# Two-layer decoder trunk on one core: first weight units by quarters, one dense step per attention turn, output norm from PSUM, four weight splits on GpSimd

## The chip, the cores and the metric

The kernel runs on one core of a Trainium2 chip. The metric is the device time of one execution in microseconds; the time before is the median of 3 runs. One further execution was taken with the hardware profiler; all rows below are of that one. Engines are named as in the profile: PE (TensorE matmul), DVE (VectorE), ACT (ScalarE), POOL (GpSimd), SP (the queue that issues the loads).

## The reference, cut to what matters

512 tokens of width 1024 pass two layers. Layer 0 mixes tokens by sliding-window attention with a learned sink per head (16 query heads, 4 key heads of 64 columns, blocks of 128 tokens; a block sees itself and the block before). Layer 1 scores keys with a small indexer (8 heads), keeps the best 128 keys per query among the causal ones, and attends to those. After each mixer comes a squared-ReLU MLP of width 4096. Each sub-layer is normed on its way in and on its way out:

```python
for layer in range(2):
    g = norm_gains[layer]
    hn = rmsnorm(x, g[0])
    mix = sliding_window_sink_attention(hn, ...) if layer == 0 else dsa_sparse_attention(hn, ...)
    x = x + rmsnorm(mix, g[1])
    hn = rmsnorm(x, g[2])
    x = x + rmsnorm(squared_relu_mlp(hn, w_mlp_up[layer], w_mlp_down[layer]), g[3])
```

Everything is float32.

## The kernel before, in words

**Products.** A float32 product is made of three matmuls on values that are split in a high and a low part (`dense`, L1396, and `three`, L1391). A *unit* is 512 rows by 512 columns of a weight matrix, 1 MB. SP loads unit `u` into one of two buffers `w_raw` (`load`, L364) and waits before that until the low part of unit `u - 2` is made. ACT makes the high part (`split`, L606), in four pieces of 512 columns with the norm's gain, or in one of 2048 where there is no gain; only after the last piece it says so, and then DVE makes the low part (`split`, L934). PE waits for `w_lo_done`. A *dense step* is one unit against one block of 128 tokens: 4 row blocks times 3 matmuls of 512 columns. Two steps (h = 0, 1) give a tile of the input projection (`in_work`, L1407) or of the output projection (`out_work`, L1443).

**Order.** Every engine has its order of work written out by hand and runs it in that order; a wait holds all that is behind it on the engine. Semaphores count what is done. SP issues the loads in the order of the units: layer 0 input projection (units 0 to 5), output projection (6 to 9), MLP (10 to 41), indexer queries (42, 43) and keys (44), layer 1 input (45 to 50), output (51 to 54), MLP (55 to 86).

**Start.** SP issues blocks 0 and 1 of x, units 0 and 1, then blocks 2 and 3 of x. PE transposes each x block (`new_x`, L1457); ACT and DVE take the high and low part (`high`, L630; `low`, L955). The first dense steps wait for the whole of unit 0. Unit 2 reuses the place of unit 0, so its split waits for unit 0's last step (`w_before`, L289; `w_spent`, L305).

**Attention.** Both layers run 16 turns (pairs of heads, one query block each) in one loop that every engine walks (`attention`, L570, L732, L1043, L1575). In turn `n` PE transposes the probabilities of turn `n - 1` (`transposes`, L1549), makes the scores of turn `n + 1` (`scores`, L1527), runs the dense steps that the table `FILL` gives to the turn (L74; steps of the input projection first, then of the output projection), turns the queries or new x blocks of the tables `Q_TURN` and `H_TURN`, and multiplies by the values (`weighted`, L1559). DVE takes in turn `n` the reciprocal of the row sums of turn `n` (`inverse`, L1031), then masks the scores of turn `n + 1` (`masked`, L1014); then come the low parts of queries and x blocks, the splits of the turn, and in layer 1 rounds of the top-k search (`more_rounds`, L1324; a round is MAX8 and MATCH_REPLACE8 over the scores). ACT copies transposed probabilities, takes the exponentials of turn `n + 1` (`expo`, L709), scales queries (`q_scaled`, L677), then high parts and splits. POOL multiplies the probabilities by the reciprocals (`normed`, L505) and rotates queries (`rope_q`, L496). The sets `{0: (5,), 5: (6,), ...}` that the three attention calls are given (L847, L919) say which unit is split at the end of which turn.

**Output norm.** After an output tile, DVE copies it out of PSUM (`y_copied`, L975), ACT squares the copy (`y_square`, L659), POOL multiplies the left half by the gain (`gained`, L513), DVE the right half (`gained`, L982), DVE adds up the squares (`mean_square`, L994), POOL takes the inverse root (`rstd_y`, L520), DVE updates X (`x_update`, L1004). After the MLP the same is done on the sum in SBUF.

**Out tail and MLP.** `out_tail` (L1624) runs the last three output tiles with `new_x` of block 2 between them; `mlp` (L1631) runs four quarters of 1024 hidden columns, the first with its up-projection in halves (`up_half`, L1637) and `new_x` of block 3 after the first of them. Between layers (L1742 to L1758) come `new_x` of blocks 1 to 3, 8 steps of indexer queries (`qi_work`), the indexer keys (`ki_work`, `ki_tokens`, `ki_back`) and the index scores (`index`).

## Time and profile before

| | |
|---|---|
| median of 3 runs | 1232.45 us (1231.23 to 1232.61) |
| the profiled execution, its own time | 1233.58 us |
| its span (first to last instruction) | 1231.8 us |
| mean granted TensorE clock | 0.968 |
| PE busy | 1133.5 us, 92% |
| DVE, ACT, POOL busy | 619.6, 452.3, 165.9 us |

A row of the timeline gives start and length in us, engine, line, operation, and in square brackets how long the engine was idle before it and what ended that. The views by stage give the busy time of each engine in a stretch and PEclk, the TensorE clock granted there as a share of the full one: 1.00 is the upper level (2.4 GHz) throughout, 0.50 would be the lower level (1.2 GHz) throughout. "Modelled ends" means that a busy PE is not always a PE at its peak. A share of busy time over the whole span mixes stages with different limits, so stages are read one at a time.

### The profile page before, as it was taken

To read this page: it belongs to the slowest core of one execution; us is meant where nothing else is said; L and a number is where in the kernel's file an instruction comes from. 1 tells how busy PE (TensorE), PEld (TensorE's weight loads), DVE (VectorE), ACT (ScalarE), POOL (GpSimd) and SP (SyncE) were. 2 spreads that over 40 slices of the span, in tenths; PEclk is the share of its full clock that TensorE was granted. 3 is DMA by queue.
4 is the path that set the end of the run, shared out by engine and by line. 5 is a ranking of instruction groups with operands and counts; after the bars stand their busy time and mean duration, and the time that the engine had idled before them with its cause. 6 is when DMAs were issued, how large, how long until landed. Compare 5 with 4: busy or idle time off the path is not lost.

```text
span 1231.8 us, 15111 instructions
## 1 busy us (share of the span) xinstructions
PE 1133.5 (92%) x5577; PEld 909.5 (74%) x5577; DVE 619.6 (50%) x1125; ACT 452.3 (37%) x854; POOL 165.9 (13%) x323
## 2 busy tenths in 40 slices
PE   4979898999999999999899848888999999999996
PEld 3867576888888888887677626555888888888885
DVE  3234553543553453557387786453552453553454
ACT  4446663323322322334454344363323221322322
POOL 0224341000000000002313222351000000000002
PEclk9989999999999999999999878899999999999999
DMA  8221411424444443443314132000515444344431
GB/s 208 65 58 34 103 35 35 103 58 113 88 101 103 102 102 84 94 96 79 86 35 99 39 88 51 1 1 5 125 43 120 103 90 103 83 101 102 103 69 68
DMA packets 50719, 97.72 MB, mean 79 GB/s; under 512 B 4384, under 2 KB 4576, under 8 KB 50656
## 3 DMA queue, kind: packets, MB, share of 16 engines
q1 hardware_dynamic: 50144, 96.78, 34.8%
q8 instruction: 38, 0.62, 0.2%
q10 hardware_dynamic: 512, 0.11, 0.1%
q14 instruction: 25, 0.20, 0.1%
HBM read 94.78 MB, written 2.10 MB: 79 GB/s over the span
## 4 chain that ended last, share of the span: by engine, by line
PE 77%; DVE 11%; ACT 6%; issue 3%; DMA 2%; POOL 1%; SPq 0%; DVEq 0%; POOLq 0%; ACTq 0%
PE bank L1393 9%; PE bank L1394 9%; PE bank L1392 9%; PE bank L1693 9%; PE bank L1692 9%; PE bank L1691 9%; PE bank L1402 6%; PE bank L1403 5%; PE bank L1404 5%; PE bank L1503 2%; PE bank L1556 2%; DVE score L1106 2%; PE bank L1570 2%; DVE top L1101 2%; DVE w_lo L951 1%
## 5 line engine op out<-in xcount | busy, mean ns | idle before, releaser
L951 DVE SCALAR_TENSOR_TENSOR w_lo<-w_raw,gT,w_hi 128x512 fp32r<-128x512 f32 x164 | 112.8, 750 | 174.3 <-ACT w_hi L626 174.2
L1691 PE MATMUL bank<-w_hi,r_hi 128*128 128x512 f32 x512 | 199.7, 390 | 0.0
L1693 PE MATMUL bank<-w_hi,r_lo 128*128 128x512 f32 x512 | 199.4, 389 | 0.0
L1692 PE MATMUL bank<-w_lo,r_hi 128*128 128x512 f32 x512 | 199.4, 389 | 0.0
L1392 PE MATMUL bank<-r_hi,w_hi 128*128 128x512 f32 (+1 forms) x456 | 178.1, 390 | 0.0
L1393 PE MATMUL bank<-r_hi,w_lo 128*128 128x512 f32 (+1 forms) x456 | 177.9, 390 | 0.0
L1394 PE MATMUL bank<-r_lo,w_hi 128*128 128x512 f32 (+1 forms) x456 | 177.9, 390 | 0.0
L626 ACT ACTIVATE w_hi<-w_raw,gT 128x512 fp32r<-128x512 f32 x164 | 105.0, 712 | 188.4 <-PE bank L1693 103.7
L941 DVE TENSOR_TENSOR w_lo<-w_raw,w_hi 128x2048 fp32r<-128x2048 f32 x36 | 82.5, 2292 | 128.6 <-ACT w_hi L618 128.6
L1402 PE MATMUL bank<-w_hi,r_hi 128*128 128x512 f32 x272 | 116.3, 427 | 16.7 <-DVE w_lo L951 9.4
L618 ACT ACTIVATE w_hi<-w_raw 128x2048 fp32r<-128x2048 f32 x36 | 68.9, 1913 | 156.1 <-PE bank L1693 118.7
L1691 PEld LDWEIGHTS bank<-w_hi,r_hi 128*128 128x128 f32 x512 | 96.4, 188 | 20.0
L1692 PEld LDWEIGHTS bank<-w_lo,r_hi 128*128 128x128 f32 x512 | 96.4, 188 | 20.0
L1693 PEld LDWEIGHTS bank<-w_hi,r_lo 128*128 128x128 f32 x512 | 96.2, 188 | 20.0
L1403 PE MATMUL bank<-w_lo,r_hi 128*128 128x512 f32 x272 | 110.6, 407 | 0.0
L1404 PE MATMUL bank<-w_hi,r_lo 128*128 128x512 f32 x272 | 110.6, 407 | 0.0
L1392 PEld LDWEIGHTS bank<-r_hi,w_hi 128*128 128x128 f32 (+1 forms) x456 | 85.5, 188 | 18.3 <-issue 0.4
L1394 PEld LDWEIGHTS bank<-r_lo,w_hi 128*128 128x128 f32 (+1 forms) x456 | 85.4, 187 | 18.3 <-issue 0.4
L1393 PEld LDWEIGHTS bank<-r_hi,w_lo 128*128 128x128 f32 (+1 forms) x456 | 85.4, 187 | 18.2 <-issue 0.4
L511 POOL TENSOR_TENSOR probs<-probs,small 128x256 f32<-128x256 f32 (+3 forms) x128 | 78.3, 643 | 112.8 <-DVE small L1034 112.7
L783 ACT ACTIVATE r_hi<-tmp_b 128x512 fp32r<-128x512 f32 x64 | 40.4, 632 | 143.6 <-DVE tmp_b L1166 143.6
L717 ACT ACTIVATE probs<-probs,small 128x257 f32<-128x257 f32 (+5 forms) x128 | 65.5, 513 | 70.1 <-DVE small L1027 69.3
(152 smaller groups left out, 1581.8 us busy)
## 6 DMA issues: line engine op xcount, KB each, us to landing
w_raw<-in_w_mlp_up SPq DMA_DIRECT2D x64, 512.0 KB, 5.9
w_raw<-in_w_mlp_down SPq DMA_DIRECT2D x64, 512.0 KB, 6.4
w_raw<-in_b_w_in SPq DMA_DIRECT2D x16, 512.0 KB, 6.1
w_raw<-in_a_w_in SPq DMA_DIRECT2D x12, 512.0 KB, 6.8
w_raw<-in_a_w_out SPq DMA_DIRECT2D x8, 512.0 KB, 5.7
w_raw<-in_b_w_out SPq DMA_DIRECT2D x8, 512.0 KB, 5.8
X<-in_x SPq DMA_DIRECT2D x4, 512.0 KB, 10.1
G<-in_norm_gains SPq DMA_DIRECT2D x4, 512.0 KB, 7.4
```

Source lines behind the costliest of these rows:

```text
L626: last = nc.scalar.activation(w_h[:, cs], w_raw[:, slot, cs], ACT.Copy, scale=gain(layer, 2 if name[:3] == "mlp" else 0, 4 * (n % 2) + k))
L941: last = nc.vector.tensor_tensor(w_l, w_raw[:, slot, :], w_h.bitcast(f32), ALU.subtract)
L951: last = nc.vector.scalar_tensor_tensor(out=w_l[:, cs], in0=w_raw[:, slot, cs], scalar=g, in1=w_h[:, cs].bitcast(f32), op0=ALU.mult, op1=A ...
L1392: nc.tensor.matmul(bank, whi, xhi, start=start, stop=False)
L1393: nc.tensor.matmul(bank, wlo, xhi, start=False, stop=False)
L1394: return nc.tensor.matmul(bank, whi, xlo, start=False, stop=stop)
L1402: nc.tensor.matmul(bank[:], xh, hi[:, k, :], start=h == 0 and k == 0, stop=False)
L1403: nc.tensor.matmul(bank[:], xh, lo[:, k, :], start=False, stop=False)
L1404: ins = nc.tensor.matmul(bank[:], xl, hi[:, k, :], start=False, stop=h == 1 and k == 3)
L1691: nc.tensor.matmul(bank[:], xh, hi[:, k, :], start=h == 0 and k == 0, stop=False)
L1692: nc.tensor.matmul(bank[:], xh, lo[:, k, :], start=False, stop=False)
L1693: ins = nc.tensor.matmul(bank[:], xl, hi[:, k, :], start=False, stop=h == 1 and k == 3)
```

## The change: what it does

1. **Start.** Units 0 and 1 are loaded and split by quarters (128 rows each, a semaphore for each); PE takes the steps of token blocks 0 and 1 quarter by quarter (`start_work`). The transposes of block 2 stand inside unit 1's steps, those of block 3 after step 4. ACT squares x blocks between the pieces.
2. **Attention.** `FILL` gives (nearly) each turn one dense step; queries and x blocks are turned right after the scores instead of before the last value product, and their high and low parts are made before the exponentials and after the first masks. DVE takes the reciprocal of turn `n + 1` at the end of turn `n`, before splits and top-k rounds, where it was the first thing in turn `n + 1`. Splits have a table (`SPLITS`), at most one a turn; unit 4's split goes behind the first queries.
3. **GpSimd** makes the low parts of layer 1's output units 51 to 54, four pieces each (`split_low`), where DVE did.
4. **Output norm.** ACT squares the output tile straight from PSUM, DVE multiplies it by the gain straight from PSUM (`out_gained`); the copy and POOL's and DVE's gain products of these tiles are gone. After the MLP, POOL makes both gain products, save one.
5. **Ends.** The out tail runs its six steps in one row, then `new_x` of block 2; `new_x` of block 3 stands inside the second `up_half`. The last down-projection finishes blocks 0 and 1 earlier. Between the layers unit 43's split (in a place of its own) goes behind two square sums on ACT and before the last X update on DVE, and the steps of indexer queries, keys and input projection are reordered.

```diff
+FILL = ({-1: (0, 1), 0: (2, 3), 1: (4,), 2: (5,), 3: (6,), 4: (7,), 5: (8,), 6: (9,), 7: (10,), 8: (11,),
+         9: (12,), 10: (13, 14), 11: (15, 16), 12: (17, 18), 13: (19,), 14: (20,), 15: (21,)},
+        {0: (0,), 1: (1,), 3: (2,), 4: (3,), 5: (4,), 6: (5,), 7: (6,), 8: (7,), 10: (8,), 11: (9,), 12: (10,), 13: (11,),
+         14: (12,), 15: (13,)})
+Q_TURN = ({-1: ((1, 0), (1, 1)), 1: ((1, 2),), 2: ((1, 3),), 4: ((2, 0),), 5: ((2, 1),), 8: ((2, 2),), 9: ((2, 3),)},
+          {-1: ((2, 0),), 0: ((2, 1),), 4: ((2, 2),), 5: ((2, 3),)})
+H_TURN = ({13: (0,), 15: (1,)}, {10: (0,), 15: (1,)})
+SPLITS = ({-1: (4,), 1: (5,), 6: (6,), 8: (7,), 9: (8,), 10: (9,)}, {1: (51,), 4: (52,), 5: (53,), 6: (54,)})
+POOL_UNITS = (51, 52, 53, 54)
...
-            load_in(0, 0)
-            load_in(0, 1)
+            for u in range(2):
+                for k in range(4):
+                    r0 = 512 * u + P * k
+                    sp.dma_start(w_raw[:, u, 512 * k:512 * k + 512], a_in[r0:r0 + P, QD:QD + 512]).then_inc(start_in[4 * u + k], 16)
...
+            def split_low(u):
+                w_h, w_l = (t.rearrange("p (k n) -> p k n", k=4) for t in w_place(u))
+                raw = w_raw[:, u % 2, :].rearrange("p (k n) -> p k n", k=4)
+                pool.wait_ge(w_hi_done, hi_no(u))
+                for k in range(4):
+                    nc.gpsimd.tensor_tensor(w_l[:, k, :], raw[:, k, :], w_h[:, k, :].bitcast(f32), ALU.subtract).then_inc(out_lo_done, 1)
...
                     if 0 <= n < TURNS:
                         normed(layer, n)
+                    for j in pending:
+                        rstd_y(norm, j)
+                    pending = []
+                    for u in SPLITS[layer].get(n - 1, ()):
+                        if u in POOL_UNITS:
+                            split_low(u)
...
                 if norm % 2:
-                    act.wait_ge(y_out, 8 * (norm // 2) + 2 * j + c + 1)
+                    d = d_no(norm // 2, "out", c, j)
+                    act.wait_ge(d_done, d + 1)
+                    v = banks[d_bank(norm // 2, d)][:]
...
+                    for c, j in Q_TURN[layer].get(n, ()) if n >= 0 else ():
+                        q_high(layer, q_no(layer, c, j))
+                    for j in H_TURN[layer].get(n, ()):
+                        high(norm, j)
                     if n + 1 < TURNS:
                         expo(layer, n + 1, 0)
                         expo(layer, n + 1, 2)
...
+            def out_gained(layer, j, c):
+                norm = 2 * layer + 1
+                dve.wait_ge(sq_done, 8 * (norm - 1) + 2 * j + c + 1)
+                dve.wait_ge(post_gain_in, 16 * norm)
                 if j >= 2:
-                    dve.wait_ge(x_new, 16 * layer + 2 * (j - 2) + c + 1)
-                nc.vector.tensor_copy(yb[:, j % 2, 512 * c:512 * c + 512], banks[d_bank(layer, d)][:]).then_inc(y_out, 1)
+                    dve.wait_ge(x_new, 8 * (norm - 1) + 2 * (j - 2) + c + 1)
+                cs = slice(512 * c, 512 * c + 512)
+                nc.vector.tensor_tensor(yb[:, j % 2, cs], banks[d_bank(layer, d_no(layer, "out", c, j))][:], G[:, cs],
+                                        ALU.mult).then_inc(y_out, 1)
...
-                    if 0 <= n < TURNS:
-                        inverse(layer, n)
                     for j in pending:
                         mean_square(norm, j)
+                    first = (0, 1, 2, 3) if n + 1 < TURNS and width(layer, turn(layer, n + 1)[1]) <= 256 else (0, 1)
                     if n + 1 < TURNS:
-                        masked(layer, n + 1)
+                        masked(layer, n + 1, first)
+                    for c, j in Q_TURN[layer].get(n, ()) if n >= 0 else ():
+                        q_low(layer, q_no(layer, c, j))
+                    for j in H_TURN[layer].get(n, ()):
+                        low(norm, j)
+                    if n + 1 < TURNS and len(first) == 2:
+                        masked(layer, n + 1, (2, 3))
                     for j in pending:
                         x_update(norm, j)
...
+                    if n == -1 and not layer:
+                        split(4)
+                    if n + 1 < TURNS:
+                        inverse(layer, n + 1)
+                    for u in SPLITS[layer].get(n, ()) if n >= 0 else ():
+                        if u not in POOL_UNITS:
+                            split(u)
                     others(n)
...
+            ROUNDS_3 = (0, 1, 3, 5, 7, 9, 11, 12, 13, 15, TOPK // 8)
...
+            def start_work():
+                for u, order in ((0, ((0, 0), (0, 1), (1, 0), (1, 1), (0, 2), (1, 2), (0, 3), (1, 3))),
+                                 (1, tuple((j, k) for j in range(2) for k in range(4)))):
...
+                        pe.wait_ge(start_lo_done, 4 * u + k + 1)
...
                     if n + 1 < TURNS:
                         scores_of(n + 1)
+                    turned(n)
                     for s in FILL[layer].get(n, ()):
                         fill(s)
                     for c in range(Ks):
-                        if c == max(0, Ks - 2):
-                            turned(n)
                         weighted(layer, n - 1, c)
...
-                    if (j, c) == (3, 0):
-                        new_x(2 * layer + 1, 2)
+                new_x(2 * layer + 1, 2)
...
+                    if end:
+                        steps = [(0, 0), (0, 1), (0, 2), (1, 0), (1, 1), (0, 3), (1, 2), (1, 3)]
...
             new_x(2, 1)
             qi_work(0, 0)
-            qi_work(0, 1)
             new_x(2, 2)
             qi_work(1, 0)
+            qi_work(0, 1)
+            qi_work(1, 1)
             new_x(2, 3)
-            qi_work(1, 1)
+            qi_work(2, 0)
             queries_turned(1, 8)
+            qi_work(2, 1)
+            queries_turned(1, 9)
             ki_work()
-            queries_turned(1, 9)
-            qi_work(2, 0)
+            qi_work(3, 0)
             ki_tokens()
-            qi_work(2, 1)
-            qi_work(3, 0)
+            qi_work(3, 1)
             queries_turned(1, 10)
             ki_back()
-            qi_work(3, 1)
+            in_work(1, 0)
             index(0)
```

## Rows read from the trace of the kernel before

**Rows 1.** The page, busy time of each engine, share of the span, instructions.
```profile
PE 1133.5 (92%) x5577; PEld 909.5 (74%) x5577; DVE 619.6 (50%) x1125; ACT 452.3 (37%) x854; POOL 165.9 (13%) x323
```

**Rows 2.** By stage: length, then busy PE, PEld, DVE, ACT, POOL, then PEclk, DMA.
```profile
0.00:94.00 94.00, 69.03 (x315) 55.25 (x316) 31.42 (x80) 43.03 (x88) 18.84 (x61) 0.95 0.47 113
94.00:186.00 92.00, 85.63 (x557) 63.06 (x556) 48.47 (x148) 58.95 (x158) 39.95 (x84) 0.98 0.23 53
186.00:230.00 44.00, 37.87 (x208) 31.66 (x207) 19.04 (x31) 15.93 (x31) 5.98 (x8) 0.92 0.21 48
230.00:560.00 330.00, 330.00 (x1514) 275.68 (x1513) 160.20 (x199) 93.20 (x120) 6.42 (x7) 1.00 0.45 97
560.00:615.00 55.00, 48.01 (x222) 37.54 (x222) 27.57 (x51) 22.94 (x49) 12.26 (x29) 0.94 0.31 72
...
689.00:848.00 159.00, 122.99 (x704) 81.82 (x702) 92.10 (x248) 78.11 (x200) 51.85 (x77) 0.87 0.12 27
848.00:881.00 33.00, 27.88 (x157) 24.52 (x156) 15.84 (x25) 11.79 (x23) 2.39 (x3) 0.95 0.27 64
...
1214.00:1231.80 17.80, 8.39 (x38) 6.60 (x36) 11.78 (x20) 2.89 (x8) 2.19 (x4) 0.83 0.31 118
```

**Rows 3.** The chain of waits: one 512-column matmul, upper clock level.
```profile
186.88 0.23 PE bank L1402
```

**Rows 4.** Timeline of the start, ACT and PE.
```profile
13.37 2.56 ACT L626 ACTIVATE w_hi<-w_raw,gT 128x512 fp32r<-128x512 f32 x4 [2.75 <-DMA w_raw<-in_a_w_in]
18.09 2.56 ACT L626 ACTIVATE w_hi<-w_raw,gT 128x512 fp32r<-128x512 f32 x4 [1.20 <-DMA w_raw<-in_a_w_in]
18.76 0.80 PE L1402 MATMUL bank<-w_hi,r_hi 128*128 128x512 f32 x1 [6.10 <-DVE w_lo L951]
30.54 1.62 PE L1469 MATMUL bank<-ident,X 128*128 128x128 f32 x8 [2.61 <-DVE r_lo L961]
```

**Rows 5.** Timeline, ACT and PE, first turn of layer 0's attention.
```profile
67.90 2.56 ACT L626 ACTIVATE w_hi<-w_raw,gT 128x512 fp32r<-128x512 f32 x4 [5.30 <-PE bank L1404]
73.97 0.47 PE L1503 MATMUL bank<-k_hi,r_hi 64*128 64x128 f32 x2 [6.17 <-DVE r_lo L972]
```

**Rows 6.** Timeline, PE, layer 0's turn 9.
```profile
136.80 2.31 PE L1556 MATMUL bank<-ident,probs 128*128 128x128 f32 x8 [3.78 <-POOL probs L511]
```

**Rows 7.** Timeline, PE, between the layers.
```profile
570.38 1.97 PE L1469 MATMUL bank<-ident,X 128*128 128x128 f32 x8 [2.31 <-DVE X L1011]
```

**Rows 8.** Groups by line, shapes apart: busy us, mean ns, idle before.
```profile
L941 DVE TENSOR_TENSOR w_lo<-w_raw,w_hi 128x2048 fp32r<-128x2048 f32 x36 | 82.5, 2292 | 128.6 <-ACT w_hi L618 128.6
L518 POOL TENSOR_TENSOR yb<-yb,G 128x512 f32<-128x512 f32 x8 | 10.3, 1284 | 47.9 <-ACT waste L668 47.9
```

**Rows 9.** Timeline, DVE, POOL and PE in one turn of layer 1.
```profile
727.79 0.18 DVE L1034 RECIPROCAL small<-small 128x4 f32<-128x4 f32 x1
728.05 2.33 POOL L511 TENSOR_TENSOR probs<-probs,small 128x256 f32<-128x256 f32 x4 [8.74 <-DVE small L1034]
730.52 1.09 PE L1556 MATMUL bank<-ident,probs 128*128 128x128 f32 x4 [6.81 <-POOL probs L511]
```

**Rows 10.** Timeline, DVE and POOL at once, then DVE alone, between the layers.
```profile
553.52 5.89 DVE L951 SCALAR_TENSOR_TENSOR early_lo<-w_raw,gT,early_hi 128x512 fp32r<-128x512 f32 x4 [0.16 <-ACT early_hi L626]
554.18 6.38 POOL L518 TENSOR_TENSOR y<-y,G 128x512 f32<-128x512 f32 x4 [269.72 <-ACT waste L668]
563.84 2.74 DVE L951 SCALAR_TENSOR_TENSOR w_lo<-w_raw,gT,w_hi 128x512 fp32r<-128x512 f32 x4 [4.42 <-ACT w_hi L626]
```

**Rows 11.** The page's groups: busy us, mean ns, the exponentials of both layers.
```profile
L717 ACT ACTIVATE probs<-probs,small 128x257 f32<-128x257 f32 (+5 forms) x128 | 65.5, 513 | 70.1 <-DVE small L1027 69.3
```

**Rows 12.** Timeline, DVE, the last norm, first and last token block.
```profile
1214.27 0.69 DVE L1177 TENSOR_TENSOR y<-y,bank 128x512 f32<-128x512 f32 x1 [9.30 <-PE bank L1693]
1225.51 0.68 DVE L1177 TENSOR_TENSOR y<-y,bank 128x512 f32<-128x512 f32 x1
```

**Rows 13.** Groups by line, shapes apart: the masks of layer 0.
```profile
L1027 DVE CUSTOM_DVE_ANT_0 probs<-bank,band,small 128x256 f32<-128x256 f32 x48 | 20.3, 478 | 8.5 <-PE bank L1503 8.5
```

More of the change, by code:

```diff
@@ L283, in w_place @@
                 return tuple(t[:] for t in early[n])
-            if name == "qi" and n == 0:
-                return tuple(t[:] for t in early[1])
-            s = {"qi": 0, "ki": 1}.get(name, u % 2)
+            if name == "qi":
+                return tuple(t[:] for t in early[1]) if n == 0 else (qi1_hi[:], qi1_lo[:])
+            s = 1 if name == "ki" else u % 2
             return w_hi[:, s, :], w_lo[:, s, :]
@@ L318, in w_spent, with hi_no, lo_no, low_of @@
             return d_done, d_no(layer, name[:-1], n // 2, 3) + 1
+        def hi_no(u):
+            return u - 1
+        def lo_no(u):
+            return u - 1 - sum(v < u for v in POOL_UNITS)
+        def low_of(u):
+            if u < 2:
+                return start_lo_done, 4 * u + 4
+            if u in POOL_UNITS:
+                return out_lo_done, 4 * POOL_UNITS.index(u) + 4
+            return w_lo_done, lo_no(u)
         def halves(w):
@@ L730, in o_high, with attention @@
                     "p (r n) -> p r n", r=4), ACT.Copy).then_inc(o_hi_done, 1)
-            def attention(layer, splits):
+            def attention(layer):
                 norm = 2 * layer + 1
@@ L740, in attention @@
                             q_high(layer, q_no(layer, c, j))
+                        for u in SPLITS[layer].get(n, ()):
+                            split(u)
                     if n == 0 and not layer:
@@ L761, in attention @@
                                 y_square(norm, j, c)
-                    for c, j in Q_TURN[layer].get(n, ()) if n >= 0 else ():
-                        q_high(layer, q_no(layer, c, j))
-                    for j in H_TURN[layer].get(n, ()):
-                        high(norm, j)
-                    for u in splits.get(n, ()):
+                    for u in SPLITS[layer].get(n, ()) if n >= 0 else ():
                         split(u)
@@ L802, in quarter @@
                             y_square(2 * layer + 2, j, 0)
-                        if not layer:
-                            split(U["qi"] + 1)
                     else:
@@ L1018, in masked @@
                 mask = own if i == 0 else score[:, i - 1, 0:W] if layer else band[:]
-                if n >= 3 or layer:
+                if es[0] == 0 and (n >= 3 or layer):
                     dve.wait_ge(pt_ready, PT_AT[N - 2])
-                for e in range(4):
+                for e in es:
                     rr, a = e // 2, e % 2
@@ L1041, in o_low, with attention @@
                                         hi.bitcast(f32), ALU.subtract).then_inc(o_lo_done, 1)
-            def attention(layer, splits, others):
+            def attention(layer, others):
                 norm = 2 * layer + 1
@@ L1081, in attention @@
                 x_update(norm, 2)
-                y_copied(layer, 3, 0)
+                out_gained(layer, 3, 0)
+                split(U[f"mlp{layer}"] + 1)
+                out_gained(layer, 3, 1)
+                mean_square(norm, 3)
                 low(norm, 2)
-                y_copied(layer, 3, 1)
-                gained(norm, 3)
-                mean_square(norm, 3)
-                split(U[f"mlp{layer}"] + 1)
                 x_update(norm, 3)
@@ L1604, in attention @@
                         turned(n)
-                    for s in FILL[layer][n][1:] if n == 0 else ():
-                        fill(s)
+                        for s in steps[1:]:
+                            fill(s)
                 for n in range(1, 17):
@@ L1649, in up_half @@
                                     h == 0 and k == 0 and m % 2 == 0, h == 1 and k == 3 and m % 2 == 1)
+                        if not half and h and n == 3:
+                            new_x(norm, 3)
                         if half and h == 0 and n == 15:
@@ L1701, in quarter @@
                         up_half(0, 0)
-                        new_x(norm, 3)
                         up_half(1, 0)
@@ L1710, in quarter @@
                     up(1, 1, it)
-                    for c in range(2):
-                        for h in range(2):
-                            for j in range(NB):
-                                down(c, h, j, it, first)
-                                if end and not layer and (c, h, j) == (1, 1, 2):
-                                    new_x(2, 0)
+                    steps = [(h, j) for h in range(2) for j in range(NB)]
+                    for h, j in steps:
+                        down(0, h, j, it, first)
+                    if end:
+                        steps = [(0, 0), (0, 1), (0, 2), (1, 0), (1, 1), (0, 3), (1, 2), (1, 3)]
+                    for h, j in steps:
+                        down(1, h, j, it, first)
+                        if end and not layer and (h, j) == (1, 2):
+                            new_x(2, 0)
                 quarter(0, True)
```

304 lines of the change are left out of this document (165 added, 139 removed).

## The prediction, made before the change was run

> **What bounds the kernel now.** First the page: PE is busy for 1133.5 of 1231.8 us [rows 1]; no other engine comes near. So I read what PE lacks, stage by stage, from the busy times by stage [rows 2]. The MLP of layer 0 (230 to 560) has PE busy all 330 us at the upper clock level, and 881 to 1214 reads the same: the change can win nothing in these 663 us. PE idles 25.0 us in the first 94, 6.4 in the rest of layer 0's attention, 6.1 in its out tail, 7.0 between the layers, 36.0 in layer 1's attention, 5.1 in its out tail and 9.4 at the end; the 3.3 that are left of 1231.8 - 1133.5 = 98.3 lie between 615 and 689. The column PEclk adds a second loss: a stage of length L at mean clock c spent 2(1-c)L at the lower level, where a matmul takes twice as long, so up to (1-c)L went there: 4.7, 1.8, 3.5, 3.3 and 1.7 us in five stages and 20.7 in layer 1's attention. These stages hold PE waits of 2 us and more [rows 4 to 7]; whether each wait that goes takes a slow stretch with it is open, so I count only part.
>
> No matmul is added or removed. The question is which waits go and which come. A dense step is 12 matmuls of 0.23 us [rows 3], 2.75 us; I use it as the measure of cover. A change under 0.2% (2.5 us) could not be told from none.
>
> **Start (0 to 94).** Units 0 and 1 land 4.7 us apart (ACT starts on them at 13.37 and 18.09 [rows 4]), so a quarter lands every 1.2 us and the first at about 9.8 (estimate). ACT needs 0.64 for a quarter, DVE 0.69 (a fourth of 2.56 [rows 4] and of 2.74 [rows 10]): the first matmul can run near 11.3 instead of 18.76, 7.4 us sooner, and six matmuls a quarter (1.4 us at the upper level, 2.8 at the lower) keep PE supplied. The 2.61 us before block 3's transposes [rows 4] go, as other steps stand there now. The 6.17 us at the first scores [rows 5] go: they were the split of unit 4, which held ACT and DVE from 67.90 with the first queries behind it, and now stands behind these. A wait comes: unit 2's split may start only after step 5, and one dense step and two key transposes (about 3.5 us) stand before its first use, where a second dense step stood too; ACT's 2.56 and then DVE's 2.74 make 5.3, so 2 us of wait. Of the clock's 4.7 I take 2. Eight DMAs instead of four on SP delay x blocks 2 and 3 by perhaps 2 us; both are needed after 20, so nothing. 7.4 + 2.6 + 6.2 - 2 + 2 = 16; bounds 10 (unit 2 twice as late, no clock) and 20.
>
> **Rest of layer 0's attention.** 3.78 us before turn 9's transposes [rows 6] come where no dense step stood in turn 8; now one stands in every turn. What is late next: at turn 9 the output projection needs the last low part of the values, which DVE makes behind unit 7's split, 2.29 us [rows 8] that wait for ACT's part first. The price lies between nothing and twice 2.29; some 3 us of PE work cover it, so I take 2. Queries turned right after the scores have one value product and one transpose less as cover: 0 to 2. Of 6.4 idle I take 4; bounds 0 and 7.
>
> **Out tails (186 to 230, 848 to 881).** The idle of 6.1 and 5.1 us [rows 2] lies where `new_x` of blocks 2 and 3 stands in PE's order while DVE and ACT still norm that block, behind a split each. Now three output tiles, 16.5 us, cover block 2, and the first `up_half` (48 matmuls at half of 0.23, 5.5 us) with the transposes covers block 3's norm, some two splits' worth (2 x 2.74 [rows 10]). That ACT and DVE read the tile in PSUM holds its bank longer, but two dense steps pass before it is needed: nothing; without them it would be the square and the product, about 1.5. Next late is block 3's update, by under 1. Of 6.1 + 3.5 I take 8 (bounds 5 and 9.6), of 5.1 + 1.7 6 (bounds 4 and 6.8).
>
> **Between the layers.** 2.31 us [rows 7]: DVE's split of unit 43 (at 563.84 [rows 10]) stood ahead of all norms; it goes behind three of them. New waits: the third indexer tile needs a bank whose eviction on ACT now stands behind block 3's high parts; the third query turn stands behind the rotation of the keys, which starts a dense step later. Each lies between nothing and a dense step, 2.75; I take 2.3 for the first, where more stands ahead, and 1.3 for the second. POOL's second gain product, 1.28 [rows 8], stands before its inverse root, where DVE took about half: 0.7. Of 7.0 + 3.3 that leaves 5; the index and top-k rounds after it are paced by DVE, so 4, bounds 1 and 8.
>
> **Layer 1's attention (689 to 848).** In turn 5 the reciprocal ran at 727.79, behind a split of 2.29 us [rows 8] and two top-k rounds; POOL had been idle 8.74, PE waited 6.81 [rows 9]. Now the reciprocal stands before both, and the four splits (4 x 2.29 = 9.2 us) leave DVE. It pays with waiting for exponentials: four take 2.05 [rows 11] while the masks run beside them, so I put 0.9 us a turn, 14 in all. DVE's 92.1 - 9.2 + 14 = 97 stays under PE's work: 41 us were at the lower level, 77% of them busy, worth 16, so 123 - 16 = 107. Walking the turns with these lengths (an estimate) I find PE still waiting for 17: 1.3 to 2 in each of the first turns, where top-k rounds stand between two masks and there is little dense work, 3.1 in turn 5 (values behind the rounds), 3.9 in turn 9. POOL takes 4 x 1.28 = 5.1 for a split and 2.33 for a turn's products [rows 8, 9], 7.4 against a turn of 6.4: units 53 and 54 come up to 3 us late, counted in the 17. Add 6 for slow clock after waits and 10 for what a walk does not find: 107 + 17 + 6 + 10 = 140 of 159, gain 19; bounds 6 (half the idle comes back) and 30.
>
> Here the trace and a rule of the Trainium skill are weighed. POOL's four products and DVE's four pieces of a split ran at once: DVE took 5.89 where it takes 2.74 alone, POOL 6.38 where four alone take 5.14 [rows 8, 10]. So each stops the other. In the turns that get POOL's splits DVE runs masks and low parts from PSUM and top-k rounds on one SBUF operand, so I add nothing. The Trainium skill, SBUF — State Buffer, "Who interferes with whom", says that a DVE instruction with two SBUF inputs and a GpSimd instruction that reads SBUF lock each other out; by that rule, X updates beside POOL's new gain products would be held, which is a rival below. The Trainium skill, GPSIMD Engine Reference, "4.1 Engine selection", speaks against the move: two-input elementwise work belongs on VectorE, being about twice as slow on GpSimd. The trace agrees, 5.14 against 2.29; the sum has that price, as POOL's time, not PE's.
>
> **End.** Token blocks cost DVE 3.75 us each in a row (1214.27 to 1225.51 for three [rows 12]) though PE ends sooner. Now blocks 0 and 1 end one dense step earlier and POOL makes three gain products: the last block starts when block 2 is done, about 1.7 sooner; bounds 0 and 2.
>
> **Sum.** 16 + 4 + 8 + 6 + 4 + 19 + 1.7 = 58.7. The profiled execution took 1233.58 us, its span 1231.8, the median 1232.45; so 1231.8 - 58.7 = 1173.1, plus 1.8 around the span, minus 1.1 from the profiled run to the median: 1174. All lower bounds together (26) give 1206, all upper ones (83) 1149.
>
> **Rivals.** (a) *DVE becomes the pacer of the turns.* It now stops for exponentials, and in out-projection turns for the dense step and the square, before the reciprocal; speaking for it are 92.1 busy us in that stage [rows 2] and the 2.05 of exponentials. If the 14 us lie on its path, layer 1 gains 5 instead of 19: 1188. (b) *The lock between DVE and POOL.* The X updates between the layers and at the end wait for the seven gain products that are new on POOL: 7 x 1.28 = 9, 1183. Against it: DVE adds from PSUM or waits for POOL's root while most of them run. (c) *Slower.* Each of 32 turns becomes a chain: masks 4 x 0.48 = 1.9 [rows 13], rest of the exponentials 0.9, reciprocal 0.2, POOL 2.33 [rows 9]; 5.3 us, of which one dense step covers 2.75: 2.55 exposed, 32 x 2.55 = 82 against 58.7 won: 1256. It decides from 1.8 us a turn. Against it: scores are a full turn ahead. (d) *Nothing gained.* Waits only move to the next semaphore: 1232. Against it: rows 4, 5 and 9 name the instruction in the way, and each is moved off.
>
> **Chances.** Forecast 0.67, (a) 0.16, (b) 0.08, (c) 0.05, (d) 0.02, better than all bounds together 0.02. The range 1154 to 1204 holds the forecast, (a) and (b) with most of their bounds and leaves out the rest and both corners. Faster by over 0.2%: 0.93; within: 0.02; slower: 0.05.
>
> **What would show it.** The stages in the new profile: first dense matmul near 11; no idle over 3 us in layer 0's turns; PE idle in layer 1's attention near 20 instead of 36 and PEclk above 0.90 there; POOL near 20 us busier; MLP stretches unchanged at 100%. I am wrong if transposes wait for POOL in most turns, if PE waits for GpSimd's low parts by more than 3 us a unit, or if idle in the first 94 us stays over 18.

## The result, and the profile after

The changed kernel takes 1166.8 us (median of 4 runs, 1165.97 to 1167.3), the kernel before 1232.53 beside it: a ratio of 0.9468, interval 0.9456 to 0.9479. 1174 was predicted, with 1154 to 1204 as the range. The profiled execution took 1166.92 us, its span is 1165.1, the mean granted clock 0.985 (before 0.968). One run of b2 below (1313.36 us) and one of the kernel before beside it (1318.3) were in a slower state and are left out of the medians and ratios given here.

The page's busy times, changed kernel; they answer to [rows 1]:

```profile
PE 1116.0 (96%) x5577; PEld 896.5 (77%) x5577; DVE 600.7 (52%) x1106; ACT 450.2 (39%) x854; POOL 192.3 (17%) x338
```

PE's busy time fell by 17.5 us though it does the same matmuls: that is slow clock that went. Its idle time fell from 98.3 to 49.1, and POOL has 26.4 us more to do. By stage (length, then busy PE, PEld, DVE, ACT, POOL, then PEclk; cut where PE's work changes), to be read beside [rows 2]:

```profile
0.00:57.00 57.00, 48.40 (x221) 39.71 (x221) 21.41 (x45) 28.32 (x52) 12.77 (x43) 1.00 0.60 159
57.00:94.00 37.00, 35.51 (x240) 26.66 (x238) 20.72 (x77) 29.22 (x83) 18.77 (x46) 1.00 0.25 57
94.00:175.00 81.00, 75.34 (x459) 54.79 (x458) 38.75 (x107) 46.80 (x119) 32.85 (x58) 0.94 0.23 53
175.00:217.00 42.00, 42.00 (x284) 38.99 (x285) 23.49 (x38) 15.78 (x29) 1.09 (x2) 1.00 0.45 98
217.00:546.00 329.00, 329.00 (x1461) 272.64 (x1461) 160.64 (x203) 96.07 (x128) 12.62 (x13) 1.00 0.42 93
546.00:600.00 54.00, 48.25 (x250) 37.10 (x248) 27.93 (x58) 26.57 (x56) 15.92 (x34) 0.97 0.40 88
600.00:657.00 57.00, 53.67 (x248) 41.82 (x244) 45.34 (x105) 24.20 (x43) 14.51 (x32) 0.97 0.33 74
657.00:790.00 133.00, 116.56 (x712) 76.89 (x711) 82.46 (x244) 78.08 (x201) 69.56 (x94) 0.95 0.14 33
790.00:831.00 41.00, 41.00 (x281) 38.12 (x280) 22.91 (x37) 15.37 (x29) 1.09 (x2) 1.00 0.45 97
```

Both out tails and the MLP are full. What PE still lacks stands in the start (5.25 of 8.6 us there ahead of the first transposes, which wait for their constants), in the second half of layer 0's turns, between the layers, and above all in layer 1's turns, where 133 - 116.56 = 16.4 us are idle (36.0 before).

Fixed points of PE's work make the two kernels comparable: the start of the first score matmul of each layer, of its last value product, and of its first whole `up` matmul, from the rows of these three lines in the trace. Between the points, in us:

| stage | before | after | won | predicted |
|---|---|---|---|---|
| start, to layer 0's first scores | 74.0 | 56.8 | 17.2 | 16 |
| layer 0's turns | 120.0 | 117.8 | 2.2 | 4 |
| layer 0's out tail | 50.2 | 41.5 | 8.7 | 8 |
| MLP, between the layers, index | 445.4 | 443.8 | 1.6 | 4 |
| layer 1's turns | 157.6 | 129.3 | 28.3 | 19 |
| layer 1's out tail | 48.6 | 41.5 | 7.1 | 6 |
| MLP and end | 336.0 | 334.4 | 1.6 | 1.7 |

(One dense step of 2.75 us stands ahead of layer 1's first scores before and behind them after; the table counts it ahead in both.) The sum is 66.7 us of span, 58.7 were forecast. Of the 28.3 us in layer 1's turns, 19.6 are idle time that went; the rest is slow clock.

A stage of one profile is not sharp to a microsecond. Layer 0's turns are the same code in the changed kernel and in e1 below; they take 117.8 and 114.8 us, with 7.15 us of idle PE in both and a granted clock of 0.957 and 0.985. So where stages of two runs are compared below, PE's idle time stands beside them.

The first dense matmul runs at 10.11 instead of 18.76 [rows 4]. Waits left on PE that the prediction had spoken of, from the timeline:

```profile
10.11 0.78 PE L1497 MATMUL bank<-w_hi,r_hi 128*128 128x512 f32 x1
...
38.87 0.50 PE L1478 MATMUL bank<-w_hi,r_hi 128*128 128x512 f32 x1 [2.35 <-DVE w_lo L1013]
...
109.94 1.02 PE L1579 MATMUL bank<-ident,qs 128*128 128x128 f32 x4 [2.11 <-POOL qs L516]
...
121.00 0.77 PE L1478 MATMUL bank<-w_hi,r_hi 128*128 128x512 f32 x1 [1.86 <-DVE r_lo L1106]
...
558.75 0.47 PE L1478 MATMUL bank<-early_hi,r_hi 128*128 128x512 f32 x1 [1.41 <-ACT qs L741]
...
579.26 0.63 PE L1579 MATMUL bank<-ident,qs 128*128 128x128 f32 x4 [2.57 <-POOL qs L516]
```

38.87 is unit 2's split, 121.00 the values' low part behind unit 7's split, 558.75 the bank of the third indexer tile, 579.26 the third indexer query: the waits that were forecast (2, 2, 2.3, 1.3). 109.94 is a query step whose rotation on POOL comes late, just above the 0 to 2 that stood there. Ahead of the first transposes PE is idle longer (5.25 us); after that the longest wait is 2.75 us at 727.16, in layer 1's turns, for DVE's masks.

### The profile page after: what moved, and what is told of

It is laid out like the page before. It is cut to its first block and busy times, and to the rows that moved or that the text cites. A ratio compares the mean times of both kernels' runs of the same rounds, so it can differ in the third digit from the quotient of the medians.

```text
span 1165.1 us, 15098 instructions
## 1 busy us (share of the span) xinstructions
PE 1116.0 (96%) x5577; PEld 896.5 (77%) x5577; DVE 600.7 (52%) x1106; ACT 450.2 (39%) x854; POOL 192.3 (17%) x338
## 5 line engine op out<-in xcount | busy, mean ns | idle before, releaser
L1789 PE MATMUL bank<-w_hi,r_hi 128*128 128x512 f32 x512 | 199.3, 389 | 0.0
L1791 PE MATMUL bank<-w_hi,r_lo 128*128 128x512 f32 x512 | 199.2, 389 | 0.0
L1790 PE MATMUL bank<-w_lo,r_hi 128*128 128x512 f32 x512 | 199.2, 389 | 0.0
L1013 DVE SCALAR_TENSOR_TENSOR w_lo<-w_raw,gT,w_hi 128x512 fp32r<-128x512 f32 x152 | 104.5, 751 | 149.3 <-ACT w_hi L678 149.2
L678 ACT ACTIVATE w_hi<-w_raw,gT 128x512 fp32r<-128x512 f32 x152 | 97.1, 713 | 174.7 <-PE bank L1791 103.7
L1003 DVE TENSOR_TENSOR w_lo<-w_raw,w_hi 128x2048 fp32r<-128x2048 f32 x34 | 78.3, 2302 | 124.7 <-ACT w_hi L670 124.7
L1478 PE MATMUL bank<-w_hi,r_hi 128*128 128x512 f32 x240 | 103.1, 430 | 8.4 <-DVE w_lo L1013 6.5
L549 POOL TENSOR_TENSOR y<-y,G 128x512 f32<-128x512 f32 x8 | 13.0, 1652 | 537.1 <-ACT waste L723 537.1
L541 POOL TENSOR_TENSOR probs<-probs,small 128x256 f32<-128x256 f32 (+3 forms) x128 | 84.4, 690 | 89.7 <-DVE small L1100 89.7
L1479 PE MATMUL bank<-w_lo,r_hi 128*128 128x512 f32 x240 | 97.6, 407 | 0.0
L1480 PE MATMUL bank<-w_hi,r_lo 128*128 128x512 f32 x240 | 97.6, 407 | 0.0
```

Of the source, the lines that this page charges most:

```text
L541: nc.gpsimd.tensor_tensor(v, v, inv_sum[:, N % 3, c:c + 1].to_broadcast([P, W]), ALU.mult).then_inc(p_done, 1)
L678: last = nc.scalar.activation(w_h[:, cs], w_raw[:, slot, cs], ACT.Copy, scale=gain(layer, 2 if name[:3] == "mlp" else 0, 4 * (n % 2) + k))
L1013: last = nc.vector.scalar_tensor_tensor(out=w_l[:, cs], in0=w_raw[:, slot, cs], scalar=g, in1=w_h[:, cs].bitcast(f32), op0=ALU.mult, op1=A ...
L1478: nc.tensor.matmul(bank[:], xh, hi[:, k, :], start=h == 0 and k == 0, stop=False)
L1479: nc.tensor.matmul(bank[:], xh, lo[:, k, :], start=False, stop=False)
L1480: ins = nc.tensor.matmul(bank[:], xl, hi[:, k, :], start=False, stop=h == 1 and k == 3)
```

## The experiments

Layer 1's turns won half as much again as forecast, so the first question is which edit did it. One edit is taken back at a time (e1, e2, e8), or made alone on the kernel before (b1, b2, b3).

**Low parts of layer 1's output units back on DVE (e1).**

```diff
-POOL_UNITS = (51, 52, 53, 54)
+POOL_UNITS = ()
```

> The changed kernel, but the low parts of layer 1's four output units go back to DVE (2.29 us each there), behind the reciprocal and ahead of the next turn's masks. Theory A (the move to POOL is worth time, because DVE paces the turns with top-k rounds, and because a two-input subtraction on DVE stops POOL, as in layer 0's turn 8, where POOL's four products took 4.37 us beside a split and 2.33 us alone): 6 to 10 us slower than the changed kernel's 1166.8, so 1173 to 1177, with POOL's products near 4.4 us in the turns that have a split. Rival B (DVE had room, the move is worth nothing): 1165 to 1169, products at 2.33.

1181.53 us, ratio to before 0.9584 (0.9568 to 0.9601): 14.7 us lost, more than even theory A had; layer 1's turns take 148.6 instead of 132.1 us from first scores to last product. DVE's four splits, with what DVE idled ahead of them (us, times), and a timeline of POOL and DVE beside the second:

```profile
L1003 DVE TENSOR_TENSOR w_lo<-w_raw,w_hi x2: 2291/2404/2517, 676.0 to 698.0; 128x2048 fp32r<-128x2048 f32 x2
L1003 DVE TENSOR_TENSOR r_lo<-w_raw,r_hi x2: 2356/2371/2386, 708.5 to 718.8; 128x2048 fp32r<-128x2048 f32 x2
...
  ACT w_hi L670: 5.5, 2
  ACT r_hi L670: 2.7, 2
```

```profile
697.74 4.38 POOL L541 TENSOR_TENSOR probs<-probs,small 128x256 f32<-128x256 f32 x4
...
697.99 2.52 DVE L1003 TENSOR_TENSOR w_lo<-w_raw,w_hi 128x2048 fp32r<-128x2048 f32 x1 [2.33 <-ACT w_hi L670]
```

The four instructions run 9.6 us, and ahead of them DVE stands 5.5 + 2.7 = 8.2 us still until ACT has made the high part: 17.8 in all. A little of that standing takes the place of other waits: from first scores to last product DVE is busy 9.6 us longer (92.0 for 82.4) and idle 6.9 us longer (56.6 for 49.7), which together are the 16.5 us that the stage lost. On PE 10.9 of them are waits (27.4 us idle for 16.4); the rest is slow clock, 0.885 granted for 0.948. POOL's four products take 4.38 us beside a split in three turns of that width and 2.33 in the one without. PE's waits in layer 1's turns, first the changed kernel, then this one (total us, times, longest):

```profile
PE bank L1599 <- DVE small L1093: 6.9, 5, 2.7
PE bank L1579 <- POOL qs L516: 2.1, 1, 2.1
PE bank L1666 <- ACT pt L778: 2.1, 3, 1.3
PE bank L1652 <- POOL probs L541: 1.6, 2, 1.2
PE bank L1478 <- POOL r_lo L562: 1.2, 1, 1.2
```

```profile
PE bank L1599 <- DVE small L1093: 15.4, 5, 4.9
PE bank L1478 <- DVE r_lo L1106: 4.8, 1, 4.8
```

PE waits for masks (L1093) and for the values' low part (L1106): work of DVE that queues behind the splits. In the changed kernel the low parts that POOL makes come late once, by 1.2 us (the last line of the first list).

**The reciprocal back in the next turn (e2).** `inverse(layer, n)` ahead of turn n+1's masks, in both layers.

> The changed kernel with the reciprocal of a turn's sums back at the start of the next turn on DVE, so behind that turn's split and top-k rounds. Theory A (the reciprocal's place is the main part of layer 1's gain): 12 to 20 us slower than the changed kernel, 1179 to 1187, with PE waiting for POOL's products in layer 1's turns. Rival C (PE's new order and one dense step a turn bring the gain, and scores a turn ahead hide the reciprocal): 1167 to 1171.

1171.98 us (0.9504; 0.9486 to 0.9522): 5.2 lost, 3.5 of it in layer 1's turns (135.6). Theory A falls here, and its rival is nearer.

**The early reciprocal alone, on the kernel before (b1).**

```diff
-                    if 0 <= n < TURNS:
-                        inverse(layer, n)
...
+                    if n + 1 < TURNS:
+                        inverse(layer, n + 1)
                     for c, j in Q_TURN[layer].get(n, ()) if n >= 0 else ():
                         q_low(layer, q_no(layer, c, j))
```

> The kernel before, with one edit alone: the reciprocal stands ahead of the queries' low parts, the splits and the top-k rounds of the turn in which its exponentials run. Theory A: 10 to 18 us faster than the kernel before, 1214 to 1222, most of it in layer 1's attention. Rival C: 0 to 4 us, 1228 to 1232. If it is slower, DVE's waits for exponentials cost more than they give without the other edits.

1232.69 us, ratio 0.9998 (0.9987 to 1.0009): nothing. PE's waits in layer 1's turns, first the kernel before, then this one:

```profile
PE bank L1556 <- POOL probs L511: 16.9, 7, 6.8
PE bank L1402 <- DVE r_lo L1040: 5.6, 2, 4.6
PE bank L1503 <- DVE small L1027: 5.4, 5, 3.0
...
PE bank L1556 <- DVE r_lo L972: 0.2, 1, 0.2
```

```profile
PE bank L1503 <- DVE small L1027: 11.0, 8, 3.1
PE bank L1556 <- DVE r_lo L972: 6.6, 1, 6.6
PE bank L1402 <- DVE r_lo L1040: 5.7, 2, 4.7
...
PE bank L1556 <- POOL probs L511: 3.8, 5, 1.2
```

The 16.9 us of waiting for POOL's products shrank to 3.8, as meant, and came back as masks (5.4 to 11.0) and as the queries' low part (0.2 to 6.6). The rest of DVE's queue came hardly sooner. In turn 5 the next masks start at 727.91 in the kernel before and at 727.25 here; behind them come the exponentials and the high and low part of a query, and PE's second transposes wait for the bank that this low part frees. First the kernel before, then b1:

```profile
731.03 0.69 DVE L972 TENSOR_TENSOR r_lo<-bank,r_hi 128x512 fp32r<-128x512 f32 x1 [1.41 <-ACT r_hi L699]
731.77 1.11 PE L1556 MATMUL bank<-ident,probs 128*128 128x128 f32 x4 [0.16 <-DVE r_lo L972]
```

```profile
730.36 0.69 DVE L972 TENSOR_TENSOR r_lo<-bank,r_hi 128x512 fp32r<-128x512 f32 x1 [0.30 <-ACT r_hi L699]
731.11 1.11 PE L1556 MATMUL bank<-ident,probs 128*128 128x128 f32 x4 [6.59 <-DVE r_lo L972]
```

The low part was as late before; the wait of 6.81 us for the products [rows 9] hid it. (In b1 the reciprocal stands ahead of the queries' low parts, in the changed kernel behind them. At this wait that costs nothing, as the low part still waits 0.30 us for ACT.)

**The old fill in layer 1 (e8).** `FILL[1]`, `Q_TURN[1]`, `H_TURN[1]` and `SPLITS[1]` of the kernel before: two dense steps in some turns, none in others.

> The changed kernel with layer 1's turns filled as in the kernel before (up to two dense steps in a turn and none in others, with the turns of queries, blocks and splits that belong to it). Theory A: 3 to 8 us slower than the changed kernel, 1170 to 1175, the idle standing in the turns without a dense step. Rival C (the even fill is the main part): 12 to 20 us slower, 1179 to 1187.

1181.86 us (0.9582; 0.9563 to 0.9601): 15.1 lost. PE waits 3.9 us for POOL's products in one turn, 3.1 for a low part from POOL, 5.1 in all for values and 8.7 in all for masks: 24.6 us idle from first scores to last product for 16.4, and PEclk is 0.89 there (0.95 with the even fill). Rival C holds.

After these four I formed theory D: DVE's queue, its waits included, paces layer 1's turns. Two edits alone on the kernel before were to test it.

**Low parts on POOL alone (b2)**: `split_low` for units 51 to 54 behind the turn's products, nothing else.

> The kernel before, with one edit alone: POOL makes the low parts of layer 1's four output units, each behind its turn's products. Theory D (formed after the first runs: DVE's queue paces layer 1's turns; a low part costs it 2.29 us and the wait for ACT's high part ahead of it, 1.0 to 3.2 us, together some 17 us for four): 8 to 16 us faster than the kernel before, 1217 to 1225. Rival E (PE waits for POOL's products, 16.9 us in that stage, and POOL gets 20 us more to do): 1232 to 1238.

**The even fill alone (b3)**: `FILL[1]`, `Q_TURN[1]`, `H_TURN[1]` and the splits' turns of the changed kernel.

> The kernel before, with one edit alone: layer 1's turns filled as in the changed kernel (one dense step in a turn, with the turns of queries, blocks and splits that belong to it). Theory D (the cover is spread better, but DVE's queue is as long as it was): 3 to 8 us faster, 1225 to 1230. Rival F (the fill is by itself worth what taking it away cost, 15 us): 1214 to 1220.

1226.03 us (0.9951; 0.9936 to 0.9967) and 1224.27 (0.9938; 0.9917 to 0.9959): 6.0 and 7.6 us won by the ratios. D's direction holds in both; its size only for the fill, and there by the ratio (the time itself is just below the 1225 to 1230). In b2 PE now waits 5.3 us for one low part from POOL and 8.3 for products: in the old fill all four units are needed within two turns. So alone the three edits are worth 0, 6.0 and 7.6 us; taken back out of the whole they cost 5.2, 14.7 and 15.1.

**All three taken back (e9)**, the edits of e1, e2 (in both layers) and e8 in one kernel.

> The changed kernel with three edits undone at once: low parts of layer 1's output units on DVE, layer 1's old fill, the reciprocal at the start of the next turn. Undone one at a time they cost 14.7, 15.1 and 5.2 us, 35.0 in sum, against 28 us that layer 1's turns won in all. If they are all of that win: 1192 to 1197, layer 1's turns as long as in the kernel before. If the new order on PE (scores and queries at the transposes) carries a part of its own: 1183 to 1191. If they add up without overlap: 1200 to 1204.

1190.33 us (0.9658; 0.9643 to 0.9673): 23.5 lost. Layer 1's turns take 153.3 us against 157.6 before, so some 4 of the 28.3 belong to the rest of the change in these turns (PE's new order and the norm from PSUM among it, not separated), and 24 to the three edits together.

**Two terms outside layer 1 (e4, e3).**

```diff
                     if n == -1:
-                        for c, j in Q_TURN[layer][n]:
-                            q_high(layer, q_no(layer, c, j))
                         for u in SPLITS[layer].get(n, ()):
                             split(u)
+                        for c, j in Q_TURN[layer][n]:
+                            q_high(layer, q_no(layer, c, j))
```

> The changed kernel with unit 4's split back ahead of the first queries on ACT and DVE. If the prediction's term is right (6.17 us of wait at the first scores were that split), 5 to 7 us slower than the changed kernel's 1166.8, so 1172 to 1174, and a wait of 5 to 6 us before the first scores. Rival (the wait only moves, unit 4 being late for its own first use): 1166 to 1168.

1173.27 us (0.9523; 0.9499 to 0.9546): 6.5 lost, and the wait is back where it was [rows 5]:

```profile
62.62 0.48 PE L1599 MATMUL bank<-k_hi,r_hi 64*128 64x128 f32 x2 [6.27 <-DVE r_lo L1034]
```

In e3 `new_x` of block 2 stands behind (3, 0), that of block 3 behind the first `up_half`, in both layers.

> The changed kernel with blocks 2 and 3 transposed at the places of the kernel before in both layers (block 2 behind two output tiles, block 3 behind the first quarter of the up projection), the norm still read from PSUM. If the prediction's term is right (the place in PE's order takes the waits), 6 to 14 us slower than the changed kernel, 1173 to 1181, in two stages. Rival (reading PSUM, without the copies, shortened the norm itself): 1166 to 1170.

1172.64 us (0.9518; 0.9482 to 0.9555): 5.8 lost, at the edge between the two. The tails take 45.4 and 43.7 us (41.5 each in the changed kernel, 50.2 and 48.6 before). Block 2's wait returns, 1.95 us in both layers, and with it slow clock; block 3's, 2.40 us before, does not, though it stands in its old place. First its row in layer 0 of the kernel before, then blocks 2 and 3 in e3:

```profile
224.51 1.10 PE L1469 MATMUL bank<-ident,X 128*128 128x128 f32 x8 [2.40 <-DVE X L1011]
```

```profile
186.76 1.65 PE L1565 MATMUL bank<-ident,X 128*128 128x128 f32 x8 [1.95 <-DVE X L1077]
...
200.54 1.03 PE L1565 MATMUL bank<-ident,X 128*128 128x128 f32 x8
```

So the places are worth 3.9 + 2.2 = 6.1 of the tails' 15.8 us; the other 9.7 come with what e3 leaves in place, the norm that reads PSUM and the new order on ACT and DVE around it; no run separates these two.

**The waits that were left (c1).** Unit 2's split gets a place that is free then, POOL makes unit 7's low part, two query steps move in each layer, unit 6's split comes a turn later, and POOL takes the third indexer query ahead of the keys:

```diff
-FILL = ({-1: (0, 1), 0: (2, 3), 1: (4,), 2: (5,), 3: (6,), 4: (7,), 5: (8,), 6: (9,), 7: (10,), 8: (11,),
+FILL = ({-1: (0, 1), 0: (2, 3), 1: (4,), 2: (5,), 3: (6,), 4: (7,), 5: (8,), 6: (10,), 7: (9,), 8: (11,),
...
-POOL_UNITS = (51, 52, 53, 54)
+POOL_UNITS = (7, 51, 52, 53, 54)
...
+            if u == 2:
+                return u2_hi[:], u2_lo[:]
...
-                        if j == 1:
+                        if j == 2:
                             rope_ki()
```

> The changed kernel with the five waits that its trace shows mended: unit 2 is split into the free place of the transposed weights, so that it needn't wait for unit 0 (PE waited 2.35 us); POOL makes unit 7's low part (two turns' products took 4.37 us beside DVE's splits, 2.33 alone, and PE waited 1.86 us for the values' low part behind it); the third query step of layer 0 is done a turn earlier and the fourth turned a turn later (2.11 and 1.04 us); POOL turns the third indexer query ahead of the keys (2.57 us); layer 1's last two queries are turned two turns later (2.11 us). If these waits stand on the path: 7 to 12 us faster than the changed kernel's 1166.8, 1155 to 1160. Rival (each wait hides another behind it, as the reciprocal alone did): 1163 to 1167.

1164.47 us (0.9445; 0.9431 to 0.9459), 2.3 us below the changed kernel, with intervals that overlap: the rival. Most of the waits moved on. PE idles 1.9 us less at the start and 1.8 less between the layers, but 2.0 more in layer 0's turns, where it now waits 2.51 us for the values' low part, 1.33 for unit 7's low part from POOL and 2.97 for unit 9's, whose load waits for that one; with 0.4 more in layer 1's turns that is 1.3 us less in all. The profiled run (1162.21, the fastest of the five) has layer 1's turns 3.5 us longer, mainly by slow clock (0.91 granted for 0.95). There PE waits for DVE:

```profile
PE bank L1602 <- DVE small L1096: 7.5, 4, 3.1
PE bank L1481 <- DVE r_lo L1109: 3.2, 1, 3.2
```

The 2.57 us ahead of the third indexer query are gone; the keys' transposes behind it wait 0.74. The mutual stop of DVE and POOL shows once more: POOL's low part of unit 7 took 7.05 us instead of 5.0, as DVE's split of unit 8 (2.57 us) ran within it:

```profile
114.94 7.05 POOL L565 TENSOR_TENSOR w_lo<-w_raw,w_hi 128x512 fp32r<-128x512 f32 x4
```

**Top-k rounds in DVE's waits (c2).** Two rounds go from ahead of the turns to turns 2 and 3, and one round stands ahead of the reciprocal, one between the halves of wide masks:

```diff
+                        others(n, 1)
                         masked(layer, n + 1, (2, 3))
...
                     if n + 1 < TURNS:
+                        others(n, 1)
                         inverse(layer, n + 1)
```

> The changed kernel with layer 1's top-k rounds placed into DVE's waits: one round between a turn's masks and its reciprocal, where DVE now waits 0.3 to 1.2 us for exponentials, in wide turns one between the two halves of the masks, where it waits 0.9 to 1.8 us for scores; two rounds ahead of the first turn go to turns 2 and 3. Theory D (DVE's queue, its waits included, paces layer 1's turns): 4 to 9 us faster than the changed kernel, 1158 to 1163, and PE's idle in layer 1's turns falls from 16.4 to 8 to 12 us. Rival (the reciprocal comes a round later, 1.2 to 1.5 us, and PE waits for the products instead): 1166 to 1171.

1161.95 us (0.9418; 0.9402 to 0.9435): 4.9 won, 2.8 of it in layer 1's turns (129.3 for 132.1), all of it idle time. Ahead of them the profiled run is 1.5 us shorter between the layers with PE's idle time the same, 9.1 us; e3 and e4, which change nothing there, are as short. PE idles 13.6 us from first scores to last product, so the count of the expectation was too hopeful, its direction right.

**Both, and the reciprocal ahead of the gain product (c3).** c1 without its edit in layer 1's turns, c2, `inverse` ahead of `out_gained` (which waits for PE's dense step and ACT's square), and `mean_square` behind the first masks.

> The changed kernel with the mended waits of the run before last (without the one in layer 1's turns, which gave nothing there) and the top-k rounds in DVE's waits, and in every turn the reciprocal ahead of the gain product that waits for PE's dense step, the mean square behind the next turn's first masks. By the stages of the two runs: 2.3 us at unit 2, 0.8 in layer 0's turns, 1.9 to 3.4 between the layers and 4.2 by the rounds, plus 0 to 3 for the reciprocal: 1154 to 1158. Rival (what is won ahead of layer 1's turns is given back in them, as in the run before last, where their stage was 3.5 us longer): 1159 to 1162.

1152.62 us (0.9362; 0.9344 to 0.9380): 14.2 us, 1.2%, below the changed kernel and better than both. It is a little more than expected: in the profiled run (1150.97, the fastest of the five) 3.0 at the start, 2.2 in layer 0's turns, 4.9 between the layers and 5.9 in layer 1's turns, 126.2 us against 129.3 in c2. Only half of it is waiting that went: PE idles 41.4 us in all for 49.1, of that 11.9 in layer 1's turns (13.6 in c2, so the two edits new in c3 took 1.8 of waits there) and 7.9 in layer 0's (0.7 more than in the changed kernel). The other half is a PE that is busy for less time, 1107.8 us for 1116.0, at a granted clock of 0.993 for 0.985. PE's waits in layer 1's turns, masks down from 6.9 to 2.5:

```profile
PE bank L1604 <- DVE small L1096: 2.5, 4, 0.9
PE bank L1671 <- ACT pt L781: 2.2, 3, 1.4
PE bank L1657 <- POOL probs L544: 1.9, 2, 1.4
PE bank L1584 <- POOL qs L519: 1.5, 1, 1.5
```

## Why the prediction was right, and where its steps were off

The time was right within 0.7%, and each stage came out faster, as forecast. The steps:

- **Start (16; 17.2).** Right, term by term: the first dense matmul 8.7 us sooner (7.4 taken), the wait at unit 2 2.35 (2 taken), unit 4's split 6.17, which e4 shows at 6.27, and PEclk 1.00 up to the first scores (0.97 in c2, whose code is the same there, for 0.2 us).
- **Rest of layer 0 (4; 2.2).** The values' low part behind unit 7's split was forecast at 2 and is 1.86. Mis-sized were the query steps, 0 to 2 together, which cost 2.11 and 1.04, and the clock: PEclk is 0.94 over the last 81 us. The clock's part differs by run, as e1's 114.8 us show.
- **Out tails (8 and 6; 8.7 and 7.1).** The sum was right, the working half right. "That ACT and DVE read the tile in PSUM ... nothing" priced a cost and saw no gain; e3 gives 9.7 of the 15.8 us to the other side of the change, and block 3's wait stays away even without the cover that the prediction counted on.
- **Between the layers (4; 1.6).** The sum has a slip: 7.0 + 3.3 less 2.3, 1.3 and 0.7 leaves 6, not 5. The wait at the third indexer tile came at 1.41 (2.3 taken); the third query turn, taken at 1.3, came at 2.57. It stands behind the keys' rotation on POOL, as was said, and that rotation has four steps of 0.65 to 0.76 us while DVE splits unit 45; the first two took 0.33 and 0.25 in the kernel before.
- **Layer 1's turns (19; 28.3).** The step that failed in size is the sum 107 + 17 + 6 + 10 = 140. Measured, with its one dense step more: 116.6 busy, of which 0.05 x 133 = 6.6 is slow clock and 2.75 the dense step, so 107 of work; 6.6 for the 6 of slow clock; 16.4 idle for the 17 of the walk. "10 for what a walk does not find" isn't there. The 17 came out partly by luck: the waits in the first turns and in turn 9 came as walked (3.9 there; 1.27 and 2.75 measured), but the 3.1 for the values in turn 5 did not, and 2.11 and 1.04 ahead of query steps, which the walk doesn't name, stand in their place. And the reasons were weighed wrongly. The prediction led with the reciprocal, and b1 shows that to be worth nothing alone, e2 5.2 us with the rest. It priced the low parts at 4 x 2.29 = 9.2 us of DVE; e1 shows 9.6 and another 8.2 in which DVE stands in its queue until ACT has the high part. And it gave the even fill no price of its own in this stage; e8 shows 15.1.
- **End (1.7; 1.6).** Right.

Of the rivals, (a), DVE as the pacer, was the nearest to the truth: the largest wait left on PE is for DVE's masks, and c2 and c3 won by using DVE's waits. It didn't decide because the low parts left DVE, with their waits. (b), the lock, exists but not at its place: the X updates take 0.74 to 0.75 us each, none stopped, and the new gain products 1.29, like the 1.28 of [rows 8]. It shows where DVE's splits run beside POOL's products and rotations: 4.4 us for 2.33 in three of layer 0's turns, and in e1 in three of layer 1's. Layer 0's three are 6 of the 26.4 us that POOL got busier, where 20 stood as a sign. (c), the serial chain, and (d) are refuted by the time, and by PE's 1.6 us of waiting for products in layer 1's turns.

The Trainium skill, SBUF — State Buffer, "Who interferes with whom", says that a DVE instruction with two SBUF inputs contends with a GpSimd instruction that reads SBUF, and that the port pair they share is an exclusive lock. The trace agrees: the split (two SBUF inputs) stopped POOL's products, 4.4 us for 2.33, and beside masks and top-k rounds four pieces of a low part took 5.0 us, no more than the 5.14 of four pieces alone [rows 8]. The Trainium skill, GPSIMD Engine Reference, "4.1 Engine selection", sends such a subtraction to VectorE; the trace agrees with its price, 5.0 against 2.3 us, and e1 disagrees with its advice here by 14.7 us: in layer 1's turns POOL had time to spare (69.6 of 132.1 us busy), and DVE's queue set the pace.

## What to carry to other kernels

A wait is named by the semaphore that came last; where one engine's queue is the pacer, moving one instruction forward in it may only change that name (b1: 16.9 us of waiting became 3.8, and the time stayed, as the rest of the queue came no sooner), and taking work out of the queue is what pays. Price work on an in-order engine with the time in which it stands at the head of its queue for its producer, not with its duration alone (9.6 us of splits made the stage 16.5 longer). Then look for the waits that are left in that queue and put work into them that nobody needs soon: c2 won 4.9 us so, and c3, with the other waits mended, 14.2, without an operation less. Count what a mended wait gives in idle time over the whole span: c1 mended five and PE idled 1.3 us less.

## What the runs showed of the hardware that was not expected

Who pays for the lock depends on the pieces. Beside one long split of DVE (128x2048) POOL loses most: 4.37 for 2.33, while DVE takes 2.65 for 2.29, in the changed kernel's layer 0:

```profile
117.38 4.37 POOL L541 TENSOR_TENSOR probs<-probs,small 128x256 f32<-128x256 f32 x4
...
117.49 2.65 DVE L1003 TENSOR_TENSOR w_lo<-w_raw,w_hi 128x2048 fp32r<-128x2048 f32 x1 [3.73 <-ACT w_hi L670]
```

In c1 POOL's four pieces of a low part lost as much to one long split, 7.05 for 5.0, and DVE took 2.57. Beside four DVE pieces of 128x512 it was DVE that lost most, 5.89 for 2.74, and POOL 6.38 for 5.14 [rows 8, 10]. So it looks as if a long instruction on DVE stops POOL for most of its length, and pieces let POOL in between; that this is the reason is inferred from these cases, and no run changed the size of the pieces, or which engine begins, alone.
